# Behind which projection of an expert pair the preceding pair's scatters and the transposes of the choice stand

## The reference

```
logits = h @ w_router ;  aff = softmax(logits)
vals, idx = top_k(aff^T, cap)            # 16 experts, each takes cap = 64 tokens
xg = h[idx]
a, u = xg @ w_e_gate, xg @ w_e_up        # 2048 -> 1024, per expert
y = (silu(a) * u) @ w_e_down * vals      # 1024 -> 2048
x = x + gt2 * scatter_add(y, idx)
```

## Time and profile before

| | before |
|---|---|
| median of 3 runs | 2184.67 us (2182.93 to 2185.39) |
| profiled execution, its own time | 2186.08 us |
| its span, first to last instruction | 2183.9 us |
| PE busy | 2100.4 us (96%) |
| VectorE busy | 891.4 us (41%) |
| ScalarE busy | 564.0 us (26%) |
| DMA moved | 634.81 MB, mean 291 GB/s |
| granted TensorE clock | 0.990 |

### The profile page before, as it was taken

How to read it: one execution, slowest core, us unless ns; L and a number is a source line. 1 busy time by engine, 2 the same in 40 slices (tenths; PEclk the granted TensorE clock), 3 DMA queues, 4 the chain that set the end, 5 groups by cost and what they waited for, 6 DMA issues and landing times.

```text
span 2183.9 us, 26204 instructions
## 1 busy us (share of the span) xinstructions
PE 2100.4 (96%) x10223; PEld 1362.0 (62%) x10223; DVE 891.4 (41%) x1270; ACT 564.0 (26%) x998; POOL 4.7 (0%) x8
## 2 busy tenths in 40 slices
PE   7999999999999999999999899999999999898987
PEld 5787888888876667888888544353534444444432
DVE  4672677766777775445333301112020302021114
ACT  4253442222246663113122501010101110011103
POOL 0000000000000000000000000000000000000000
PEclk9999999999999999999999999999999999999998
DMA  9947675887860002434422899999999999999998
GB/s 364 370 180 283 246 254 194 326 310 284 293 219 25 25 1 88 153 125 150 153 87 77 335 397 404 428 426 427 427 427 426 429 427 427 427 427 427 426 422 308
DMA packets 144064, 634.81 MB, mean 291 GB/s; under 512 B 11987, under 2 KB 29545, under 8 KB 112757
## 3 DMA queue, kind: packets, MB, share of 16 engines
q1 hardware_dynamic: 139348, 625.38, 73.1%
q10 hardware_dynamic: 4640, 8.40, 1.0%
HBM read 621.15 MB, written 12.58 MB: 290 GB/s over the span
## 4 chain that ended last, share of the span: by engine, by line
PE 81%; DMA 13%; DVE 4%; ACT 2%; issue 1%; SPq 0%; DVEq 0%; ACTq 0%
PE bank L812 24%; PE bank L1319 23%; PE bank L814 14%; DMA e_wide<-in_w_e_up 12%; PE bank L1291 5%; PE bank L872 3%; PE bank L998 3%; PE bank L1091 2%; PE bank L1311 1%; DMA e_slot<-in_w_e_down 1%; ACT probs_m L1691 1%; PE bank L1301 1%; PE bank L1312 1%; DVE nmax L2238 1%; PE bank L1079 1%
## 5 line engine op out<-in xcount | busy, mean ns | idle before, releaser
L1319 PE MATMUL bank<-e_wide,xgT 128*64 128x512 f32 x1456 | 407.0, 609 | 42.2 <-DMA e_wide<-in_w_e_up 27.2
L1500 ACT ACTIVATE w_hi<-stage 128x1024 fp32r<-128x1024 f32 (+1 forms) x168 | 175.4, 1044 | 588.4 <-PE bank L812 333.2
L1925 DVE TENSOR_TENSOR w_lo<-stage,w_hi 128x1024 fp32r<-128x1024 f32 (+1 forms) x168 | 202.4, 1205 | 291.7 <-ACT w_hi L1500 290.3
L1319 PEld LDWEIGHTS bank<-e_wide,xgT 128*64 128x64 f32 x1456 | 132.1, 140 | 285.9 <-issue 285.0
L1319 PE MATMUL bank<-e_slot,xgT 128*64 128x512 f32 x584 | 208.0, 600 | 0.0
L1319 PE MATMUL bank<-e_wide,heT 128*64 128x512 f32 x672 | 167.4, 594 | 0.0
L812 PE MATMUL bank<-hT_hi,w_hi 128*128 128x512 f32 x512 | 159.0, 392 | 0.0
L812 PE MATMUL bank<-hT_lo,w_hi 128*128 128x512 f32 x512 | 157.8, 389 | 0.0
L812 PE MATMUL bank<-hT_hi,w_lo 128*128 128x512 f32 x512 | 157.7, 389 | 0.0
L2507 DVE TENSOR_TENSOR x<-x,bank 128x512 f32<-128x512 f32 x128 | 79.7, 683 | 191.0 <-PE bank L1312 189.4
L2000 DVE SCALAR_TENSOR_TENSOR ada_acc<-ada_tile,siluc,ada_acc 128x1024 f32<-128x1024 f32 x116 | 148.7, 1282 | 8.1 <-DMA ada_tile<-in_w_ada 2.5
(11 more groups left out here) (365 smaller groups left out, 2946.3 us busy)
## 6 DMA issues: line engine op xcount, KB each, us to landing
e_wide<-in_w_e_up SPq DMA_DIRECT2D x49, 2048.0 KB, 17.2
e_wide<-in_w_e_gate SPq DMA_DIRECT2D x42, 2048.0 KB, 15.5
e_wide<-in_w_e_down SPq DMA_DIRECT2D x42, 2048.0 KB, 17.2
ada_tile<-in_w_ada SPq DMA_DIRECT2D x156, 512.0 KB, 6.2
stage<-in_w_in SPq DMA_DIRECT2D x96, 512.0 KB, 6.9
e_slot<-in_w_e_gate SPq DMA_DIRECT2D x43, 1024.0 KB, 16.4
e_slot<-in_w_e_down SPq DMA_DIRECT2D x41, 1024.0 KB, 17.1
e_slot<-in_w_e_up SPq DMA_DIRECT2D x30, 1024.0 KB, 10.2
```

What stands on the lines that cost most here:

```text
L1319: last = mm(acc[h][64 * e:64 * e + 64, :], stationary(e), weights(h, e), start=first, stop=end)
L1500: A(w_hi[:, c % NSPLIT, :, 0:width], stage[:, c % NSTAGE, :, 0:width], ACT.Copy).then_inc(hi_ready, 1)
L1925: V.tensor_tensor(w_lo[:, c % NSPLIT, :, 0:width], stage[:, c % NSTAGE, :, 0:width], w_hi[:, c % NSPLIT, :, 0:width].bitcast(F32), ALU.sub ...
```

## The change

For every pair but the first, the four scatters of the preceding pair move from behind the w_gate steps to behind the w_up steps. `selection(p)` moves from behind the first w_up step to behind the last scatter, after a wait until VectorE has added all four scattered quarters. On ScalarE the two sigmoids move ahead of the roundings of quarters 2 and 3; on VectorE the two products with the sigmoid move ahead of the first `add_scattered`. Nothing is added to or taken from the work. Pair 0 keeps its order.

```diff
@@ pe_pair, all pairs but the first
                         up_wide(p, 2 * g, 0, g)
-                        if g == 0:
-                            pe.wait_ge(xg_ready, STEPS + 4 * p)
-                        scatter(p - 1, g)
                     for g in range(KG):
                         if g == 0:
                             pe.wait_ge(y32_ready, 4 * p)
                         up_wide(p, 2 * KG + 2 * g, 2, g)
                         if g == 0:
-                            pe.wait_ge(scat_added, 16 * p)
-                            selection(p)
+                            pe.wait_ge(xg_ready, STEPS + 4 * p)
+                        scatter(p - 1, g)
+                    pe.wait_ge(scat_added, 16 * p)
+                    selection(p)
@@ act_pair
+            def gate_sigmoids(p):
+                act.wait_ge(e_used, EC * p + 2 * STEPS)
+                for j in range(2):
+                    A(sg[:, j, :], bank[j][:, :], ACT.Sigmoid).then_inc(sgm_ready, 1)
                         y_round(p - 1, jd)
                         if jd == 1:
                             tokens(p, 3, 5)
-                act.wait_ge(e_used, EC * p + 2 * STEPS)
-                for j in range(2):
-                    A(sg[:, j, :], bank[j][:, :], ACT.Sigmoid).then_inc(sgm_ready, 1)
+                            gate_sigmoids(p)
+                if first:
+                    gate_sigmoids(p)
@@ y_added, dve_pair
+            def gated(p):
+                for j in range(2):
+                    dve.wait_ge(sgm_ready, 2 * p + j + 1)
+                    V.tensor_tensor(sg[:, j, :], bank[j][:, :], sg[:, j, :], ALU.mult).then_inc(silu_ready, 1)
                 y_rest(p, 0)
                 y_rest(p, 1)
+                gated(p + 1)
                 add_scattered(p, 0)
...
-                if not first:
+                if first:
+                    gated(p)
+                else:
                     y_added(p - 1)
-                for j in range(2):
-                    dve.wait_ge(sgm_ready, 2 * p + j + 1)
-                    V.tensor_tensor(sg[:, j, :], bank[j][:, :], sg[:, j, :], ALU.mult).then_inc(silu_ready, 1)
```

## The result

The changed kernel takes 2217.32 us (median of 4 runs, 2216.55 to 2217.55) against 2185.03 us before (4 runs, 2182.93 to 2185.76). The ratio is 1.015 (95% interval 1.0138 to 1.0162): 32.3 us slower, where 20.4 us were forecast (2205 us) with 2213 us as the upper end. The sign, the place and the causes came out as forecast, the size did not: the part of TensorE's clock was put far too low.

What follows compares the result with a forecast made beforehand. Weight transfers were taken to bound the kernel. Six pairs' late release 12.6, clock 2.7 and tail 5.1 us gave 20.4 us slower, 2205 us, with an 8 in 10 range of 2190 to 2213 us.

Steps and rivals of the forecast that it cites:

- the ring's reach: At the first w_down step's end, three-step weight ring: queue holds work for 6.8 us behind the issue, a pair's tightest point.
- Parts 1 and 2: Scatters leaving w_gate gain nothing; scatters between w_up steps cost zero, hidden by the wait for weights.
- Part 3: Last scatter and selection ahead of gather(4, 0): 6.1 us later, 2.1 us lost per pair, 12.6 us in six.
- the one case at 1358: Pair 1's first w_gate step before the change: transfers issued as the queue ran empty, landing 7.7 and 12.6 us after issue.
- the rival drawn from the Trainium skill: Quicker restart of the empty queue: 1.1 us lost per pair, 14.4 us in all, 2199.1 us; chance 0.10.
- Part 4: TensorE at 1.2 GHz behind the selection: 0.6 us in six pairs and the tail, 1.5 us less elsewhere, together +2.7.
- The upper sum: Slow clock in nearly every pair at 3.8 us each, plus the tail: 28.1 us, 2212.8 us; chance 0.05.
- Part 5: Last pair's w_down starts later behind adds, selection and val, and TensorE carries it to the end: +5.1 us in full.
- the covered ring: The ring bridges the pairs and mainly the tail is paid: 3.6 up to 10 us, 2188.3 to 2194.7 us; chance 0.20.
- not slower: Ring bridges each pair and the last pair's w_down is bound by its transfers: 2183.2 us; chance 0.08.
- The slow stretch falls into nearly every pair: TensorE's slow clock behind the selection in nearly all pairs, 3.8 us lost in each: 28.1 us, 2212.8 us; chance 0.05.

Runs made afterwards that it cites:

- e3: Kernel before, plus seven matmuls that nobody reads ahead of gather(4, 0) in pairs 1 to 6; 2203.67 us, ratio 1.0083.
- e5: Kernel before, plus three matmuls that nobody reads ahead of gather(4, 0) in pairs 1 to 6; 2185.03 us, ratio 1.0003.
- e6: Kernel before, plus ten matmuls that nobody reads ahead of gather(4, 0) in pairs 1 to 6; 2218.31 us, ratio 1.0158.
- e4: Kernel before, with scatters behind w_gate's third and fourth and w_up's first two steps, selection behind w_up's third; 2183.83 us, ratio 0.9999.
- e11: The change on TensorE alone, with ScalarE and VectorE in the order of the kernel before; 2217.19 us, ratio 1.0146.
- e1: Changed kernel, plus five small matmuls that nobody reads in each of the two waits around the selection; 2202.49 us, ratio 1.0084.
- e2: Changed kernel, with the last pair alone in the order of before on TensorE, ScalarE and VectorE; 2213.01 us, ratio 1.0133.
- e7: Kernel before, with scatters behind w_gate's fourth and w_up's first three steps, only the selection behind the last w_up step; 2190.28 us, ratio 1.0024.
- e9: Changed kernel, with a pair's four gathers spread one behind each w_down step; 2220.56 us, ratio 1.0166.
- e12: e1 with each pair's second gather moved from ahead of the first w_down step to behind the second, two more small matmuls; 2202.56 us, ratio 1.0084.

## Why the prediction was wrong in its size

- **What bounds, and the ring's reach.** Right. The loads set the period, the place with the least to spare is the first w_down step, and the queue bears about 4 us there (6.8 us of data were counted behind the issue; e3, e5 and e6 measure what can be used of them).
- **Parts 1 and 2, scatters out of w_gate and into w_up at no cost.** Right: e4, and e11 for ScalarE and VectorE.
- **Part 3, 6.1 us later and 2.1 us lost.** Right in the wait (6.04 us) and nearly right in the loss: e1, which has this term alone, loses 2.5 us in a pair, 15.2 us in the six where 12.6 were forecast. The landings of 7.7 and 11.7 us are those of the one case at 1358 that the forecast leaned on (7.7, and 12.6 us for both; here 1565.02 + 11.7 - 1564.16 = 12.6). With that the rival drawn from the Trainium skill, "DMA: Bandwidth & Descriptors", "Latency and other measured facts", is out: both transfers by 11.6 us was an estimate from its figures. That page of the Trainium skill fits its fixed cost and its rate to transfers issued by GpSimd, and those here are issued by SyncE.
- **Part 4, the clock: the step that failed.** I took "a third, 0.6" us of a slow stretch of at most 1.7 us. The runs show 2.2 us in a pair (e1 against the changed kernel, by their traces), nearly four times as much, and 1.4 us in the tail. Two things were mis-sized. First, the chance: the stretch came in each of the six pairs. Second, the bound: the gather took 6.78, 6.46, 6.68 and 6.79 us in pairs 1 to 4 and 5.27 and 5.47 us in pairs 5 and 6, so in four of six TensorE stayed at 1.2 GHz for nearly twice as long as in any row of before, and lost 2.7 to 3.0 us, not 1.7. Against 3.77 us the six gathers are 14.8 us longer together, of which e1's pairs gave back 13.5. Nearly all of it fell beyond the ring's reach, since the wait of 6.1 us had used that up already. The upper sum of 28.1 us held the chance right and the bound wrong.
- **Part 5, the tail.** 4.4 us by the traces; e2 gives 3.7 to 4.3. With the clock's 0.6 added and the 1.5 us of the last w_up step taken off (7.09 us now, 8.61 before) 4.2 were forecast. That this is so near is in part luck: e1 has 2.9 us where the forecast without the clock had 3.6, and the clock cost 1.4 us where it had 0.6.
- **The sum.** Forecast for the six pairs 12.6 + 3.6 = 16.2 us, measured 28.7. Of the excess of 12.5 us the clock is 13.5 - 3.6 = 9.9 and the wait 15.2 - 12.6 = 2.6.

Of the rivals, the covered ring and "not slower" are out by e3 and e2. "The slow stretch falls into nearly every pair", with a chance of 0.05, is the one that came, and its price was still too low: 28.1 us forecast, 32.3 measured.

## What to carry to other kernels

Where a ring of transfers sets the pace, ask of every edit when each buffer is released, not how busy the engine is: this change moved 6 us of work and waits to ahead of the one release that had 4 us to spare, and paid for the excess of 2 us, and for the slow clock on top of it, in every pair. The same work one step earlier was free (e4), and with one scatter moved away again it cost 6 us and not 32 (e7). A release's lateness has to be added up over all that follows, with the waits that the moved work used to cover (e9, e12). And the chain of short waits and small matmuls cost twice here, once as waits and once as the slow clock behind it; a few matmuls without a use in the waits took back almost half of this loss.

## What the runs showed of the hardware

- Waits of 1.18 and 1.34 us with 1.45 us of small matmuls between them were followed by 1.2 GHz in every one of six pairs, twice as long in four of them as in any pair of the kernel before. The same two waits filled with ten 128-column matmuls left the gather at full speed (3.84 us). The small matmuls with the second wait alone (e7) were followed by 1.2 GHz in four of six pairs.
- 4 MB of weights, issued when the queue is empty or about to be, have landed 12.6 us after the first issue (seen at 1358.27 before, one transfer of 2 MB and two of 1 MB, and at 1564.16 after, two of 2 MB), against 9.81 us for the same bytes in a full queue.
- The edge is not sharp. At a release gap of 19.6 to 19.7 us the loads behind the first w_down step lost 0.4 to 0.6 us in four pairs of e7 and 0.0 to 1.1 us in the six of e12, by their landings.
